# First expert with two weight splits ahead of its tokens, unread products around the choice of experts, raw-token queries

## The reference

```python
# layer 0
h = rmsnorm(x, ev_mix_norm)            # x * rsqrt(mean(x*x) + eps) * w
x = x + even_mixer(h, ...)             # its first step: proj = h @ w_in, (1024 x 3072): q, k, v | r, k, v
x = x + swiglu(rmsnorm(x, ev_ffn_norm), ...)
# layer 1
x = x + odd_mixer(rmsnorm(x, od_mix_norm), ...)   # ends in concat([y_c, y_d]) @ w_out
h = rmsnorm(x, od_ffn_norm)
probs = softmax(h @ router)            # 8 experts
top_p, top_i = top_k(probs, 2); top_p = top_p / sum(top_p)
for e in range(8):
    out = out + gates[..., e:e + 1] * swiglu(h, w_gate[e], w_up[e], w_down[e])   # 1024 x 3584
```

## Time and profile before

| | us |
|---|---|
| runs, median of 3 | 1687.97 (1687.21 to 1689.55) |
| profiled execution | 1687.32 |
| its span | 1685.6 |
| TensorE busy in the span | 1645.2 (98%) |
| VectorE, ScalarE busy | 1248.7 (74%), 987.2 (59%) |

### The profile page before, as it was taken

The page is one execution under the profiler, slowest core; times in us unless marked ns, Lnnn a source line. Parts: engine busy times, 40 slices in busy tenths (PEclk is TensorE's granted clock), DMA queues, the critical chain, the costliest instruction groups (busy, mean ns, idle before and its releaser), DMA issues.

```text
span 1685.6 us, 22093 instructions
## 1 busy us (share of the span) xinstructions
PE 1645.2 (98%) x8492; PEld 1356.5 (80%) x8492; DVE 1248.7 (74%) x1205; ACT 987.2 (59%) x958; POOL 87.4 (5%) x106
## 2 busy tenths in 40 slices
PE   7999999999999999799999999999999999999997
PEld 3868995999988885688888888888888888888886
DVE  5578555445423763688988988988988988989886
ACT  2356333434443432577777777777777777777774
POOL 2005230000000030000000000000000000000000
PEclk9999999999999999799999999999999999999999
DMA  6311014455443211799999999999999999999993
GB/s 244 106 52 50 2 51 150 151 199 187 147 173 118 103 48 66 272 398 365 358 378 371 341 370 379 341 384 361 356 372 359 365 368 363 361 363 364 366 370 129
DMA packets 200948, 434.11 MB, mean 258 GB/s; under 512 B 10906, under 2 KB 34734, under 8 KB 200878
## 3 DMA queue, kind: packets, MB, share of 16 engines
q1 hardware_dynamic: 199438, 427.90, 70.1%
q0 software_dynamic: 1440, 5.24, 0.8%
HBM read 431.02 MB, written 2.10 MB: 257 GB/s over the span
## 4 chain that ended last, share of the span: by engine, by line
PE 91%; DVE 5%; issue 2%; ACT 2%; DMA 0%; SPq 0%; DVEq 0%; ACTq 0%
PE bank L2724 17%; PE bank L2726 16%; PE bank L2725 16%; PE bank L2504 5%; PE bank L2435 4%; PE bank L2434 4%; PE bank L2433 4%; PE bank L2009 3%; PE bank L2022 2%; DVE split L1944 2%; PE bank L2199 2%; PE bank L2667 2%; PE bank L2403 2%; PE bank L2222 2%; PE bank L2787 1%
## 5 line engine op out<-in xcount | busy, mean ns | idle before, releaser
L1944 DVE TENSOR_TENSOR split<-ring,split 128x2048 fp32r<-128x2048 f32 x336 | 762.1, 2287 | 107.2 <-ACT split L1149 105.4
L1149 ACT ACTIVATE split<-ring 128x2048 fp32r<-128x2048 f32 x336 | 640.3, 1925 | 174.4 <-PE bank L2726 174.4
L2724 PE MATMUL bank<-split 128*128 128x512 f32 x896 | 355.3, 397 | 5.7 <-DVE split L1944 5.7
L2726 PE MATMUL bank<-split 128*128 128x512 f32 x896 | 350.5, 391 | 0.0
L2725 PE MATMUL bank<-split 128*128 128x512 f32 x896 | 349.3, 390 | 0.0
L2724 PEld LDWEIGHTS bank<-split 128*128 128x128 f32 x896 | 168.7, 188 | 39.2 <-issue 5.8
L2726 PEld LDWEIGHTS bank<-split 128*128 128x128 f32 x896 | 168.4, 188 | 36.4
L2725 PEld LDWEIGHTS bank<-split 128*128 128x128 f32 x896 | 168.9, 189 | 33.7
L2724 PE MATMUL bank<-split,ehr_ 128*128 128x512 f32 x448 | 181.9, 406 | 4.4 <-DVE split L1944 4.4
L2726 PE MATMUL bank<-split,ehr_ 128*128 128x512 f32 x448 | 175.7, 392 | 0.0
L2725 PE MATMUL bank<-split,ehr_ 128*128 128x512 f32 x448 | 175.0, 391 | 0.0
(11 more groups left out here) (486 smaller groups left out, 1955.7 us busy)
## 6 DMA issues: line engine op xcount, KB each, us to landing
ring<-in_od_moe_gate SPq DMA_DIRECT2D x112, 1024.0 KB, 7.2
ring<-in_od_moe_up SPq DMA_DIRECT2D x112, 1024.0 KB, 7.5
ring<-in_od_moe_down SPq DMA_DIRECT2D x112, 1024.0 KB, 6.9
ring<-in_od_w_in SPq DMA_DIRECT2D x7, 2048.0 KB, 7.6
ring<-in_ev_w_in SPq DMA_DIRECT2D x6, 2048.0 KB, 9.0
ring<-in_ev_ffn_gate SPq DMA_DIRECT2D x11, 1024.0 KB, 5.2
ring<-in_ev_ffn_up SPq DMA_DIRECT2D x11, 1024.0 KB, 7.8
ring<-in_ev_ffn_down SPq DMA_DIRECT2D x5, 2048.0 KB, 7.8
```

The lines of the kernel that those rows point to most:

```text
L1149: act.activation(wst[:, r % NSTAGE, 0, :], ring[:, (r % NHALF) * HALF:(r % NHALF + 1) * HALF], ACT.Copy).then_inc(w_hi, 1)
L1944: dve.tensor_tensor(wst[:, r % NSTAGE, 1, :], ring[:, (r % NHALF) * HALF:(r % NHALF + 1) * HALF], wst[:, r % NSTAGE, 0, :].bitcast(F32), S ...
L2724: pe.matmul(o, hi, wh, start=start, stop=False)
L2726: return pe.matmul(o, lo, wh, start=False, stop=stop)
```

## The change

- Start: TensorE transposes `x_sb` itself as soon as it lands (`raw_tokens`), and `xrT` gets it times the norm's weight, without `rstd`. Queries and keys are computed from `xrT`; `rstd` of the token enters as the scale of `qkv_copy`. The first weight load is issued as two transfers, of four column tiles each, and the query products run in two halves over them. The transposes of `xn` stand between queries and keys, into banks 4 to 7; `hT` is copied from there and serves the raw columns. VectorE's vector sums (`cmix`) come behind `xn`, its half of `hT` behind the masks.
- Choice of experts: `router_tokens(1)` comes ahead of `logits(0)`. `unread(n)` is a product of the identity with n mask columns into bank 1, which nobody reads: one of 512 ahead of `router_tokens(1)`, 512 and 256 behind `logits(1)`, 256 behind the rank products. The `sem_inc` of `half_ps` moves up to right behind `logits(1)`.
- First expert: weight halves 0 and 1 are split ahead of the weighing and splitting of the tokens, on ScalarE and VectorE.

```diff
...
@@ -224,6 +224,7 @@
         sw, lora = g_g.take(2, 4, SEQ), g_g.take(3, SEQ)
+        xrT = mix[:, 0:KT, :]
         g_g2 = Region(arena, 0, 11272)
...
@@ -529,6 +531,9 @@
                 for dst, src in parts:
+                    if (kind, n) == ("ev_in", 0):
+                        sp.dma_start(dst[:, 0:4, :], src[:, 0:4, :]).then_inc(w0_in, 16)
+                        dst, src = dst[:, 4:8, :], src[:, 4:8, :]
                     sp.dma_start(dst, src).then_inc(landed[s], 16)
@@ -713,6 +718,17 @@
                 act.wait_ge(act_chain, chain[0])
+
+            def qkv_copy(i, bank):
+
+                act.wait_ge(qkv_ps, i + 1)
+                if i < 4:
+                    act.wait_ge(xn_rdy, i % 2 + 1)
+                    act.activation(qkv[:, i % 2, 512 * (i // 2):512 * (i // 2) + 512], B[bank][:, :], ACT.Copy,
+                                   scale=rstd[:, i % 2:i % 2 + 1]).then_inc(qkv_sb, 1)
+                else:
+                    act.activation(qkv[:, i % 2, 512 * (i // 2):512 * (i // 2) + 512], B[bank][:, :],
+                                   ACT.Copy).then_inc(qkv_sb, 1)
 
@@ -737,6 +753,20 @@
                     act.wait_ge(dve_const, DVE_CONST["cols"])
+                    for half in range(2):
+                        act.wait_ge(pe_step, PE_STEPS["xr0_ps" if half == 0 else "xr1_ps"])
+                        for k in range(4 * half, 4 * half + 2):
+                            last = act.activation(xrT[:, k, :], B[k // 2][:, SEQ * (k % 2):SEQ * (k % 2) + SEQ], ACT.Copy,
+                                                  scale=cols[:, COL[name] + k:COL[name] + k + 1])
+                        last.then_inc(act_step, 1)
+                    for i in range(2):
+                        qkv_copy(i, i)
+                    for k in range(KT // 2):
+                        act.wait_ge(xnT_ps, k // 2 + 1)
+                        last = act.activation(hT[:, k, :], B[4 + k // 2][:, SEQ * (k % 2):SEQ * (k % 2) + SEQ], ACT.Copy,
+                                              scale=cols[:, COL[name] + k:COL[name] + k + 1])
+                    last.then_inc(hT_act, 1)
+                    return
                 if ni == 1:
...
@@ -774,7 +799,7 @@
 
-            for i in range(4):
+            for i in range(2, 4):
                 qkv_copy(i, i)
@@ -1140,6 +1165,8 @@
                     for r in range(PER + 1):
+                        if first and r == 2:
+                            split_tokens(ps, 0, 0)
                         for what, j in duties[r]:
@@ -1151,7 +1178,6 @@
 
-                    split_tokens(ps, 0, 0)
                     expert(ps, 0, 0)
@@ -1206,13 +1232,23 @@
             dve.wait_ge(dve_const, DVE_CONST["cols"])
+            mw = COL["ev_mix_norm"]
+            for half in range(2):
+                dve.wait_ge(pe_step, PE_STEPS["xr0_ps" if half == 0 else "xr1_ps"])
+                for k in range(4 * half + 2, 4 * half + 4):
+                    last = dve.tensor_scalar(xrT[:, k, :], B[k // 2][:, SEQ * (k % 2):SEQ * (k % 2) + SEQ],
+                                             cols[:, mw + k:mw + k + 1], None, MUL)
+                last.then_inc(dve_step, 1)
+            for a in range(TT):
+                dve.wait_ge(std_rdy, a + 1)
+                link(dve.reciprocal(rstd[:, a:a + 1], std[:, a:a + 1]))
+                dve.tensor_scalar(xn[:, a, :], x_sb[:, a, :], rstd[:, a:a + 1], None, MUL).then_inc(xn_rdy, 1)
             mu, lm = COL["ev_shift_mu"], COL["ev_lora_mu"]
             dve.scalar_tensor_tensor(cmix[:, 0:12], cols[:, mu:mu + 12], -1.0, cols[:, mu + 12:mu + 24], MUL, SUB)
             dve.scalar_tensor_tensor(cmix[:, 12:20], cols[:, lm:lm + 8], -1.0, cols[:, lm + 8:lm + 16], MUL, SUB)
             ka = COL["ev_k_a"]
             link(dve.tensor_scalar(cmix[:, 20:24], cols[:, ka:ka + 4], -1.0, None, MUL))
             link(dve.tensor_scalar(cmix[:, :], cmix[:, :], 1.0, None, ADD))
-            norm(0, "ev_mix_norm")
 
@@ -1234,6 +1270,14 @@
             dve.wait_ge(dve_const, DVE_CONST["mask"])
+
+            for k in range(KT // 2, KT):
+                dve.wait_ge(xnT_ps, k // 2 + 1)
+                last = dve.tensor_scalar(hT[:, k, :], B[4 + k // 2][:, SEQ * (k % 2):SEQ * (k % 2) + SEQ],
+                                         cols[:, mw + k:mw + k + 1], None, MUL)
+            last.then_inc(hT_dve, 1)
+            dve.wait_ge(hT_dve, 1)
+            dve.wait_ge(hT_act, 1)
 
@@ -1937,6 +1981,9 @@
                     for r in range(PER + 1):
+                        if at == 0 and r == 2:
+                            weigh_tokens(ps, 0, 0)
+                            split_tokens(ps, 0, 0)
                         for what, j in duties[r]:
@@ -1946,8 +1993,6 @@
 
-                    weigh_tokens(ps, 0, 0)
-                    split_tokens(ps, 0, 0)
                     expert(ps, 0, 0)
@@ -1997,22 +2042,55 @@
 
+            def raw_tokens(a):
+                pe.wait_ge(x_in[a], 16)
+                for k in range(KT):
+                    last = pe.transpose(B[k // 2][:, SEQ * (k % 2) + P * a:SEQ * (k % 2) + P * a + P],
+                                        x_sb[:, a, P * k:P * k + P], ident[:, :])
+                    if a == TT - 1 and k % 4 == 3:
+                        last.then_inc(pe_step, 1)
+
             pe.wait_ge(ident_rdy, 1)
+            raw_tokens(0)
             pe.wait_ge(vec_in, 32)
             pe.transpose(B[7][:, 0:N0], vecrows[0:N0, 0, :], ident[0:N0, 0:N0])
             pe.transpose(B[7][:, P:P + N1], vecrows[0:N1, 1, :], ident[0:N1, 0:N1]).then_inc(vec_tp, 1)
-            norm(0)
-            pe.wait_ge(dve_const, DVE_CONST["cols"])
+            raw_tokens(1)
+
             def tile_in(n, a, bank):
                 w8 = weights("ev_in", n).rearrange("p (k n) -> p k n", k=KT)
+                h = xrT if n < 2 else hT
                 for k in range(KT):
-                    last = pe.matmul(B[bank][:, :], hT[:, k, P * a:P * a + P], w8[:, k, :],
+                    last = pe.matmul(B[bank][:, :], h[:, k, P * a:P * a + P], w8[:, k, :],
                                      start=(k == 0), stop=(k == KT - 1))
                 last.then_inc(qkv_ps, 1)
 
-            def tokens_in(n, banks):
+            s = where["ev_in", 0][0]
+            w8 = ring[:, s * SLOT:(s + 1) * SLOT].rearrange("p (k n) -> p k n", k=KT)
+            pe.wait_ge(w0_in, 16)
+            for half in range(2):
+                if half:
+                    weights("ev_in", 0)
+                pe.wait_ge(act_step, ACT_STEPS["xr1_act" if half else "xr0_act"])
+                pe.wait_ge(dve_step, DVE_STEPS["xr1_dve" if half else "xr0_dve"])
                 for a in range(TT):
-                    tile_in(n, a, banks[a])
+                    for k in range(4 * half, 4 * half + 4):
+                        last = pe.matmul(B[a][:, :], xrT[:, k, P * a:P * a + P], w8[:, k, :],
+                                         start=(k == 0), stop=(k == KT - 1))
+                    if half:
+                        last.then_inc(qkv_ps, 1)
+            pe.wait_ge(dve_const, DVE_CONST["cols"])
+            for a in range(TT):
+                pe.wait_ge(xn_rdy, a + 1)
+                for k in range(KT):
+                    last = pe.transpose(B[4 + k // 2][:, SEQ * (k % 2) + P * a:SEQ * (k % 2) + P * a + P],
+                                        xn[:, a, P * k:P * k + P], ident[:, :])
+                    if a == TT - 1 and k % 2:
+                        last.then_inc(xnT_ps, 1)
+            for a in range(TT):
+                tile_in(1, a, 2 + a)
+            pe.wait_ge(hT_act, 1)
+            pe.wait_ge(hT_dve, 1)
 
@@ -2023,8 +2101,6 @@
 
-            tokens_in(0, (0, 1))
-            tokens_in(1, (2, 3))
             for m in range(4):
@@ -2678,6 +2754,10 @@
 
+                def unread(n):
+                    pe.matmul(B[1][:, 0:n], ident[:, :], smask[:, 0].rearrange("p m s -> p (m s)")[:, 0:n],
+                              start=True, stop=True)
+
                 def logits(n):
@@ -2705,11 +2785,15 @@
                 od_half(1, 1, 1)
+                unread(512)
+                router_tokens(1)
                 logits(0)
-                router_tokens(1)
             if UPTO >= 4:
 
                 logits(1).then_inc(pe_step, 1)
+                pe.sem_inc(half_ps, NSTAGE)
+                unread(512)
+                unread(256)
                 pe.wait_ge(dve_step, DVE_STEPS["as_rdy"])
@@ -2851,7 +2936,6 @@
 
-                pe.sem_inc(half_ps, NSTAGE)
                 all_experts(0)
```

More of the change, by code:

```diff
@@ L53 @@
 ACT_STEPS = {n: i + 1 for i, n in enumerate(
-    "sin_rdy qk_std kk_std ln1_std ln0_std ba_sb sp_l ge_rdy on_std rt_exp".split())}
+    "xr0_act xr1_act sin_rdy qk_std kk_std ln1_std ln0_std ba_sb sp_l ge_rdy on_std rt_exp".split())}
 DVE_CONST = {n: i + 1 for i, n in enumerate("eps cols mask".split())}
 DVE_STEPS = {n: i + 1 for i, n in enumerate(
```

(5 more changed lines are left out.)

## The result

| | before | after |
|---|---|---|
| runs, median | 1687.59 (1685.51 to 1689.55) | 1673.70 (1673.51 to 1675.42) |
| profiled execution | 1687.32 | 1673.59 |
| its span | 1685.6 | 1671.9 |
| mean granted clock | 0.991 | 0.996 |

The ratio is 0.9919, with a 95% interval from 0.9904 to 0.9935: 13.7 us less, 11.0 to 16.2. The prediction was 1678.4, from 1674.5 to 1684.0. One execution of the front alone (1849.95 us) and one of the kernel before beside it (2802.37 us) were in a much slower state and are in no ratio.

What follows compares the result with a forecast made beforehand. TensorE was taken as the bound, so only its idle or slow stretches count. Front 2.2 us plus back 7.4 made 9.6 us off 1687.32, 1677.7, plus 0.65 to the median: 1678.4 us, range 1674.5 to 1684.0.

Steps and rivals of the forecast that it cites:

- Bound: Whole kernel: TensorE is 91% of the last-ending chain, so whatever is gained before the first expert reaches the end.
- Start of the queries: Front: query products start at 9.9 us instead of 14.6, when half the weights land; 4.7 us gained.
- Clock in front: First query products: early transposes taken as no help to the array's clock; 0.3 us of loss.
- rival A: Transposes wake the array, which stays awake over 3.0 us at the first expert: 13.1 us gained, 1674.9; 15%.
- Logits and choice: Choice of experts: logits behind token turns with unread products, logits(1) at full speed until 676.2; gain 1.9 us.
- Gather: Behind the rank products: starts at 681.2 and runs at full speed, 3.9 us, ending at 685.1 instead of 689.44.
- First expert product: First expert: two weight splits ahead of the tokens bring the product at 688.1, 7.0 us earlier.
- Slow products behind it: First seven expert products, 0.43 us apart before: between 0 and 1.5 us saved, taken as 0.4.
- B: Clock falls at the logits anyway: front 2.2 us, back 4.1 to 5.6, time about 1680.9; 15%.
- C: Front: both half loads land together at 12.5, so the front gives -0.2 us; 1680.8; 6%.
- D: Expert loops: loads, not TensorE, pace the experts, so the back's gain is lost; only 2.2 us, 1685.8; 5%.
- E: Expert loops: 4032 split products each slow by 5 ns in another rhythm, 20 us lost; 1698.4; 4%.

Runs made afterwards that it cites:

- front alone: The kernel before with only raw-token queries, two half loads and moved transposes: 1685.63 us, ratio 0.9986.
- doubled transposes: The kernel before with the 16 transposes of the normed tokens done twice, nothing else added: 1688.44 us, ratio 1.0003.
- three more waits filled: The changed kernel with unread 512-column products ahead of and behind the FFN norm's transposes and ahead of the last down products: 1673.85 us, ratio 0.9923.
- second measurement: The changed kernel unaltered, measured again beside three of the experiments: 1675.86 us, ratio 0.9934.
- back alone: The kernel before with only the edits around the choice of experts and in the first expert: 1677.40 us, ratio 0.9938.
- logits ahead of the turns: The changed kernel with logits(0) ahead of the second token turns again, unread products kept: 1677.69 us, ratio 0.9945.
- splits alone: The kernel before with only the two weight splits ahead of the first expert's tokens and the stage count behind the logits: 1681.50 us, ratio 0.9965.

## Why the prediction was right and wrong

The forecast gain was 9.6 us, and the spans of the two profiles differ by 13.7 (13.9 by the aligned products). What was missing is 2.45 us of the clock in front, 1.0 of slow products at the first expert, 0.7 of the fixed work in front and 0.3 of that in the back; the parts that the change doesn't touch give -0.1 together (-1.3, -0.4 and 1.6). The steps that failed are therefore the two terms of the clock: 0.3 us of loss in front, on the ground that transposes are no help, where this execution gained 2.15; and 0.4 us at the first expert, where all of it came. The product times are those of one execution; the other three have only their times on record.

- **Bound.** Right: the array is still busy for 836 of 840 us in the expert loops, and the lead behind the first expert's slow products is kept to the last down products within 0.4 us.
- **Start of the queries.** Forecast 9.9, measured 9.67 to 10.6 over the profiles with the half loads. In most of them the chain goes through the landing of the first half; in the changed kernel's it goes through ScalarE's copy of the raw tokens, which ended at 9.67. Transposes between queries and keys: forecast 2.2, measured 1.75.
- **Clock in front.** Here the sum said 0.3 us of loss, and the profiled execution had the 2.15 us of gain of rival A: the clock rose at the end of the raw transposes, at 8.3 us. The reason given for the term, that transposes are no help, is refuted by the run with doubled transposes. How much the early ones help differs by execution, since the wait for the weights comes behind them: against the 16.1 us of the first 32 passes before the change, the seven profiles of this front without filler lie between 2.15 us of gain and 0.85 of loss, 0.6 of gain in the middle. The front alone gave 2.4 us (0.8 to 4.0) against 2.2 forecast; that total holds the clock's falls elsewhere too, and doesn't make the term right.
- **Logits and choice.** Forecast 1.9 us up to the rank products, measured 5.87 - 3.99 = 1.9. Gather starts 2.5 us earlier, forecast 2.3.
- **Gather.** Forecast 3.9 us, measured 5.45: wrong as to the clock, while 3.81 in the profile with three more waits filled shows that the work was sized rightly. The clock fell as it began, behind the choice, in the profiles of the changed kernel (677.3), of its second measurement (678.4) and of the back alone (681.6), and in others already within the choice (at 673.65 with the logits ahead of the turns). The slow gather cost only 0.3 us, as VectorE's two splits end at 681.5 anyhow, one microsecond ahead of it.
- **First expert product.** Forecast 7.0 us, measured 7.3 in the profiles of the changed kernel and of the back alone. In the forecast VectorE's queue is late last; in both of these the gather was, behind VectorE by 1 us, and the two came out nearly the same.
- **Slow products behind it.** This term was mis-sized: I took 0.4 us, and it was the whole, 1.4 by the aligned products. The pause was 1.4 us, not 3.0, because the slow gather filled it: I had set the pause by the fast one. But that isn't all of it, for with a fast gather and a pause of 2.75 us the products behind were not slow either (three more waits filled).
- **Untouched parts.** They had no term. I let the clock vary only in the two stretches that are edited. But the clock falls in other pauses too, and not in the same ones in every execution: 1.3 us lost behind the FFN's norm, 1.6 won at the last down products, in the control 1.1 lost at 478. None of these was in the sum or the bounds, which makes the range too narrow; yet in this pair they nearly cancel, so they are not what carried the time below it. Beside rival A's 13.1 us, which the range was to take in, it was the 0.7 of fixed work in front, 0.2 in the back, and 0.5 from the step between one execution and the median, which I took at 0.65 us and which was 0.1 after the change.
- **Last down products.** They ran slowly in all four profiles whose logits stand in the old order without unread products (kernel before, front alone, splits alone, doubled transposes) and in one of the ten others (logits ahead of the turns). Whether the edits have a part in that, or chance alone, no run shows.
- **Rivals.** A came nearest to the first measurement (13.1 us), and by its front mechanism for that execution. B's back is what the splits alone do (5.7 against 4.1 to 5.6). C is excluded. D and E are excluded: the lead stays constant within 0.4 us from the first expert to the last.

Not settled: why the first measurement gave 13.7 us and the second 11.1. Of the first four executions three took 1673.5 to 1673.8 us, the fourth 1675.42 at a lower mean clock; only one of them is profiled, and of the second six only one of the two fastest (1674.59). The intervals overlap, and chance isn't told apart from something in that chip's timing of the first loads. By the second measurement the prediction would have been inside its range, with the same terms wrong.

## What to carry to other kernels

When two streams must both be ready, put first the one whose inputs are there already: two weight splits moved ahead of tokens that were still being gathered gave 4 us and cost nothing. A pause on the array can cost twice, once as a pause and once in the products behind it. Cheap products that nobody reads can spare the second; here they held the clock over the logits but not up to the gather, and they paid only together with the new order of the logits, 2.9 us as a pair and at most 0.3 each. So test two such edits apart and together before dropping one. For a change of a few microseconds, look at several profiles of one kernel before believing one: the ten executions of this one, unaltered, spread from 1673.51 to 1678.10 us, a third of its gain.

## What the runs showed of the hardware

- Transposes raise TensorE's clock like products: 16 of them took 3.56 us at the start of their run and the next 16 took 1.9, with nothing else between (the kernel with doubled transposes; its record of the clock has the first rise at 12.9 us, and no product came before 16.4).
- One kernel, unaltered, rose to full speed at 8.3 us in one execution and at 12.8 in another, with the first query product at the same place within 0.1 us (9.65 and 9.74).
- The clock fell with pauses well below the 5.6 us that I had before me: with 1.45 and 0.63 us close together, in all six profiles that came to them at full speed (677.3 in the changed kernel's), and with 1.77 and 2.06 around a set of transposes (284.8). The latter passed without a fall in other executions (before the change, around 290), and so did 2.75 us behind a gather at full speed (three more waits filled).
